# Two layer programs, each with its norms, MLP and projections, in place of nine barriered stages

## What is computed

```python
for layer in range(2):
    sh1, sc1, g1, sh2, sc2, g2 = ada(c, w_ada[layer], b_ada[layer])
    if layer == 1:
        kv = x @ w_kv                       # written out as k and v
    h = x * (1 + sc1) + sh1
    mix = pool_mixer(h) if layer == 0 else stick_breaking(h @ w_q, keys, vals) @ w_o
    x = layer_norm(ALPHA * x + g1 * mix)
    h = x * (1 + sc2) + sh2
    f = square(relu(h @ w_up[layer])) @ w_down[layer]      # 1024 -> 4096 -> 1024
    x = layer_norm(ALPHA * x + g2 * f)
```

## Time and profile before

| | |
|---|---|
| median of 3 runs | 3626.75 us (3626.16 to 3627.1) |
| the profiled execution's own time | 3627.95 us, its span 3626.2 us |
| PE busy | 3166.2 us (87% of the span) |
| DVE busy | 1961.4 us (54%) |
| ACT busy | 923.5 us (25%) |
| POOL busy | 445.2 us (12%) |

### The profile page before, as it was taken

One profiled execution on the slowest core, in us unless ns is written; L12 is line 12 of the kernel. 1 busy time (PEld: TensorE's weight loads), 2 busy tenths in 40 slices (PEclk: granted clock), 3 DMA queues, 4 the chain that ended last, 5 costly groups with the idle time before them and its releaser, 6 DMA issues. The chain is left out here.

```text
span 3626.2 us, 56133 instructions
## 1 busy us (share of the span) xinstructions
PE 3166.2 (87%) x20656; PEld 2672.9 (74%) x20656; DVE 1961.4 (54%) x3395; ACT 923.5 (25%) x1598; POOL 445.2 (12%) x248
## 2 busy tenths in 40 slices
PE   5664999999995997799899997888794999999997
PEld 1234999999994997765565654444493999999995
DVE  2566555555555112266666666888615555555554
ACT  0114000000003002144444445777504000000003
POOL 0002111212210111100000000000010221222210
PEclk8887999999997998899999998999997999999998
DMA  8711111111100221399999993000001111111101
GB/s 329 254 48 58 41 35 46 38 43 46 40 23 29 80 78 52 127 380 404 395 397 398 397 408 103 24 24 18 24 23 29 47 41 46 46 46 46 46 23 49
DMA packets 215691, 433.75 MB, mean 120 GB/s; under 512 B 13664, under 2 KB 130057, under 8 KB 212441
## 3 DMA queue, kind: packets, MB, share of 16 engines
q1 hardware_dynamic: 215521, 431.67, 32.8%
...
## 5 line engine op out<-in xcount | busy, mean ns | idle before, releaser
L84 PE MATMUL bank<-hi,mlp_uphi 128*128 128x364 f32 (+1 forms) x1536 | 506.5, 330 | 92.5 <-POOL mlp_uplo L692 92.5
L85 PE MATMUL bank<-lo,mlp_uphi 128*128 128x364 f32 (+1 forms) x1536 | 506.6, 330 | 0.0
L86 PE MATMUL bank<-hi,mlp_uplo 128*128 128x364 f32 (+1 forms) x1536 | 506.4, 330 | 0.0
L85 PE MATMUL bank<-mlp_flo,mlp_dnhi 128*128 128x364 f32 (+1 forms) x1536 | 504.8, 329 | 0.0
L84 PE MATMUL bank<-mlp_fhi,mlp_dnhi 128*128 128x364 f32 (+1 forms) x1536 | 504.7, 329 | 0.0
L86 PE MATMUL bank<-mlp_fhi,mlp_dnlo 128*128 128x364 f32 (+1 forms) x1536 | 504.7, 329 | 0.0
L302 DVE SCALAR_TENSOR_TENSOR x_t<-bank,mod,x_t 128x364 f32<-128x364 f32 (+1 forms) x432 | 245.6, 571 | 379.0 <-PE bank L86 376.7
L84 PEld LDWEIGHTS bank<-hi,mlp_uphi 128*128 128x128 f32 x1536 | 290.4, 189 | 93.6 <-POOL mlp_uplo L692 93.6
L1291 PE MATMUL bank<-ident,sa_kraw 128*128 128x128 f32 x2048 | 278.7, 281 | 58.5 <-DMA sa_kraw<-in_cache_k 53.5
L1291 PEld LDWEIGHTS bank<-ident,sa_kraw 128*128 128x128 f32 x2048 | 225.8, 142 | 111.2 <-DMA sa_kraw<-in_cache_k 83.0
L1173 DVE COPY sa_kt<-bank 128x512 f32<-128x512 f32 x256 | 177.0, 692 | 215.6 <-PE bank L1291 211.7
...
## 6 DMA issues: line engine op xcount, KB each, us to landing
sa_kraw<-in_cache_k SPq DMA_DIRECT2D x256, 512.0 KB, 10.6
sa_vpage<-in_cache_v SPq DMA_DIRECT2D x256, 512.0 KB, 9.4
mlp_raw<-in_w_up SPq DMA_DIRECT2D x64, 512.0 KB, 4.0
mlp_raw<-in_w_down SPq DMA_DIRECT2D x64, 512.0 KB, 3.5
...
pm_wada<-in_w_ada SPq DMA_DIRECT2D x48, 512.0 KB, 5.2
...
```

The costliest lines, as they stand in the source:

```text
L84: pe.matmul(out, w_hi, x_hi, start=start, stop=False, skip_group_check=True)
L85: pe.matmul(out, w_hi, x_lo, start=False, stop=False, skip_group_check=True)
L86: return pe.matmul(out, w_lo, x_hi, start=False, stop=stop, skip_group_check=True)
```

## The change

Query projection and attention are kept as they were. The other nine stages after the pool mixer become two programs, `first_layer_mlp` (n00, m0, n01, keys and values) and `second_layer_mlp` (wo, n10, m1, n11, the output), each one block with one barrier at its end. `norm` becomes a class whose steps are single calls per piece: `pe_mean`, `dve_center`, `act_square`, `pe_var`, `dve_scale`, `act_root`, `act_high` (writes `hi` and the full h from `x_t` with gain, bias and modulation folded into `coef`), `dve_split` (writes `lo`), `act_affine`. DVE's steps are done in two halves of 4 chunks. `Mlp` takes the norm before it and the norm after it and calls their steps inside its first and its last block. The up jobs are in another order (`UP`), wo goes by pieces with all its weights held, the keys and values take two weight blocks in turn by token tiles, and the norms use PSUM banks 6 and 7.

The diff, cut to its core:

```diff
+    def pe_mean(self, pe, s):
+        c0, w = PIECES[s]
+        if s == 2:
+            pe.wait_ge(self.centred, 4)
+        for m in range(NC):
+            last = pe.matmul(self.mean_bank[s][:, 0:w], self.k.mean_of[:, :], self.k.x_t[:, m, c0:c0 + w],
+                             start=(m == 0), stop=(m == NC - 1))
+        last.then_inc(self.mu, 1)
+    def pe_var(self, pe, s):
+        c0, w = PIECES[s]
+        if s == 1:
+            pe.wait_ge(self.root, 1)
+        else:
+            pe.wait_ge(self.centred, 2 * s + 2)
+        for m in range(NC):
+            if m % 4 == 0:
+                pe.wait_ge(self.squared, 2 * s + m // 4 + 1)
+            last = pe.matmul(self.var_bank[s][:, 0:w], self.k.mean_of[:, :], self.sq[:, m, c0:c0 + w],
+                             start=(m == 0), stop=(m == NC - 1))
+        last.then_inc(self.var, 1)
...
+    def dve_center(self, dve, s):
+        w = PIECES[s][1]
+        dve.wait_ge(self.mu, s + 1)
+        for half in range(2):
+            x = self.piece(self.k.x_t, s, half)
+            dve.tensor_tensor(x, x, self.mean_bank[s][:, 0:w].unsqueeze(1).to_broadcast([P, 4, w]), ALU.subtract
+                              ).then_inc(self.centred, 1)
+    def dve_scale(self, dve, s):
+        w = PIECES[s][1]
+        v = self.var_bank[s][:, 0:w]
+        dve.wait_ge(self.var, s + 1)
+        dve.tensor_scalar(v, v, EPS, None, ALU.add).then_inc(self.eps, 1)
+        dve.wait_ge(self.eps, s + 1)
+        dve.reciprocal(v, v).then_inc(self.inv, 1)
+        dve.wait_ge(self.root, s + 1)
+        for half in range(2):
+            x = self.piece(self.k.x_t, s, half)
+            dve.tensor_tensor(x, x, self.rstd[:, 0:w].unsqueeze(1).to_broadcast([P, 4, w]), ALU.mult
+                              ).then_inc(self.scaled, 1)
...
+    def act_root(self, act, s):
+        w = PIECES[s][1]
+        act.wait_ge(self.inv, s + 1)
+        if s:
+            act.wait_ge(self.scaled, 2 * s)
+        act.activation(self.rstd[:, 0:w], self.var_bank[s][:, 0:w], ACT.Sqrt).then_inc(self.root, 1)
...
+    def act_high(self, act, s):
+        k = self.k
...
+                else:
+                    scale, shift = k.coef[:, m:m + 1], k.coef[:, 8 + m:9 + m]
+                    act.activation(k.hi[:, m, c0:c0 + wp], x, ACT.Identity, bias=shift, scale=scale)
+                    last = act.activation(self.h[:, m, c0:c0 + wp], x, ACT.Identity, bias=shift, scale=scale)
+            last.then_inc(self.high, 1)
...
+    NB, FC, JOBS, BANKS, TILES = DFF // 512, 4, 36, 6, 8
+    ORDER = [("down", 0), ("up", 2), ("down", 1), ("up", 3), ("down", 2), ("down", 3), ("next", 0), ("next", 1)]
+    UP = [(0, 0), (0, 1), (1, 0), (1, 1), (0, 2), (1, 2), (2, 0), (2, 1), (2, 2), (3, 0), (3, 1), (3, 2)]
...
+    def act_rest(self, act):
+        def hi_half(i, r, kind, c):
+            used = {"down": 0, "up": 3 + c, "next": 9 + 3 * (c % 2)}[kind]
+            act.wait_ge(self.raw_in[r % 2], i * (self.TILES // 2 * 16) + 16 * ((2 + r) // 2 + 1))
+            act.wait_ge(self.job_done, i * self.JOBS + (used + 1))
+            act.activation(self.split_target(kind, c)[0], self.raw[:, r % 2, :], ACT.Copy).then_inc(self.w_hi_done, 1)
...
+        def block(i, first=False, last=False):
+            own.base, own.k = i * (36 + 16), 0
+            for j, (c, s) in enumerate(self.UP):
+                c0, w = PIECES[s]
+                if first and j == 2:
+                    before.dve_split(dve, 2)
+                dve.wait_ge(self.job_done, i * self.JOBS + (j + 2))
...
+            dve.wait_ge(self.bank_free, i * self.JOBS + (self.BANKS + 12))
+            if first:
+                dve.wait_ge(before.normed, 3)
+            for j in range(12, self.JOBS):
+                s, m = divmod(j - 12, NC)
+                dve.wait_ge(self.job_done, i * self.JOBS + (j + 2))
+                gated_add(dve, own, k, self.layer, 5, m, s, k.ps[j % self.BANKS], self.tmp, self.bank_free)
+                if last and s and m == 1:
+                    after.dve_center(dve, s - 1)
+                if last and s == 2 and m == 2 and after.to:
+                    after.dve_split(dve, 0)
+                if last and s and m == 6:
+                    after.dve_scale(dve, s - 1)
+        block(0, first=True)
+        with dve.Fori(1, self.NB - 1) as i:
+            block(i)
+        block(self.NB - 1, last=True)
...
+        def block(i, first=False, last=False):
+            for j in range(self.JOBS):
+                pe.wait_ge(self.bank_free, i * self.JOBS + (j + 1))
+                if j < 12:
+                    c, s = self.UP[j]
+                    c0, w = PIECES[s]
+                    if s == 0:
+                        pe.wait_ge(self.w_done, i * self.TILES + (2 + (1, 2, 4, 6)[c]))
+                    if first and c == 0:
+                        pe.wait_ge(before.split, s + 1)
...
+                done.then_inc(self.job_done, 1)
+                if first and j == 1:
+                    before.pe_var(pe, 2)
+                if last and j in (12 + 8 + 1, 12 + 16 + 1):
+                    s = (j - 12) // 8 - 1
+                    pe.wait_ge(self.bank_free, i * self.JOBS + (self.BANKS + 12 + 8 * s + 8))
+                    after.pe_mean(pe, s)
+                if last and j in (12 + 8 + 5, 12 + 16 + 5):
+                    after.pe_var(pe, (j - 12) // 8 - 1)
+        block(0, first=True)
+        with pe.Fori(1, self.NB - 1) as i:
+            block(i)
+        block(self.NB - 1, last=True)
+        pe.wait_ge(self.bank_free, self.NB * self.JOBS + self.BANKS)
+        after.pe_mean(pe, 2)
...
+    JOBS = ([(0, t) for t in range(5)] + [(1, t) for t in range(5)] + [(0, t) for t in range(5, 9)]
+            + [(1, t) for t in range(5, 9)])
...
+        def high_weights(act, i, n):
+            act.wait_ge(raw_in[n], i * 16 + 16)
+            act.wait_ge(job_done, i * 18 + (14 + 4 * n))
+            act.activation(weights(0, n), raw[:, n, :, :], ACT.Copy).then_inc(w_hi_done, 1)
...
+        @block.sync
+        def _(sp):
+            ff.sync(sp)
...
+            sp.wait_ge(ff.job_done, ff.jobs_until(11))
+            for n in range(2):
+                load(sp, n, slice(n * W, (n + 1) * W))
...
+            ff.act_first(act)
+            n0.act_square(act, 0)
+            n0.act_square(act, 1)
+            n0.act_root(act, 0)
+            n0.act_high(act, 0)
+            n0.act_square(act, 2)
+            n0.act_root(act, 1)
+            n0.act_high(act, 1)
+            n0.act_root(act, 2)
+            n0.act_high(act, 2)
+            n0.act_affine(act, 2)
+            n0.act_affine(act, 0)
+            n0.act_affine(act, 1)
+            ff.act_rest(act)
+            for s in range(3):
+                n1.act_square(act, s)
+                if s:
+                    act.wait_ge(ff.job_done, ff.jobs_until(12 + 8 * s + 7))
+                    high_weights(act, 0, s - 1)
+                n1.act_root(act, s)
+                n1.act_high(act, s)
+                n1.act_affine(act, s)
...
+        @block.vector
+        def _(dve):
+            n0.dve_coefficients(dve)
+            n0.dve_center(dve, 0)
+            n0.dve_center(dve, 1)
+            n0.dve_scale(dve, 0)
+            n0.dve_center(dve, 2)
+            n0.dve_scale(dve, 1)
+            n0.dve_split(dve, 0)
+            n0.dve_split(dve, 1)
+            n0.dve_scale(dve, 2)
+            ff.dve(dve)
+            n1.dve_center(dve, 2)
+            n1.dve_split(dve, 1)
+            for j in range(3):
+                keep(dve, 0, j)
+            n1.dve_scale(dve, 2)
+            for j in range(3, 8):
+                keep(dve, 0, j)
+            n1.dve_split(dve, 2)
+            for j in range(8, 18):
+                keep(dve, 0, j)
+            with dve.Fori(1, 4) as i:
+                for j in range(18):
+                    keep(dve, i, j)
...
+            n0.pe_mean(pe, 0)
+            n0.pe_mean(pe, 1)
+            n0.pe_var(pe, 0)
+            n0.pe_mean(pe, 2)
+            n0.pe_var(pe, 1)
+            ff.pe(pe)
+            for j in range(18):
+                if j in (0, 2, 10):
+                    pe.wait_ge(n1.split, (0, 2, 10).index(j) + 1)
+                if j == 3:
+                    n1.pe_var(pe, 2)
+                job(pe, 0, j)
+            with pe.Fori(1, 4) as i:
+                for j in range(18):
+                    job(pe, i, j)
...
+            for j in range(24):
+                s, m = divmod(j, NC)
+                c0, w_ = PIECES[s]
+                if s == 0:
+                    pe.wait_ge(w_done, m + 1)
+                if j >= BANKS:
+                    pe.wait_ge(bank_free, j - BANKS + 1)
...
+                if s and m == 1:
+                    pe.wait_ge(bank_free, NC * s)
+                    n0.pe_mean(pe, s - 1)
+                if s and m == 3:
+                    n0.pe_var(pe, s - 1)
+            pe.wait_ge(bank_free, 24)
+            n0.pe_mean(pe, 2)
+            ff.pe(pe)
+            pe.wait_ge(n1.normed, 1)
```

(38 more changed lines are left out.)

668 lines of the change are left out of this document (340 added, 328 removed).

## The result

The changed kernel takes **3543.14 us** (median of 4 runs, 3540.34 to 3548.3) against 3626.45 before; the ratio is 0.9772, 95% interval 0.9755 to 0.9789. The profiled execution is the slowest of the four, 3548.3 us with a span of 3546.6.

A forecast was written before the change was run, and what follows sets the result against it. TensorE was taken to bound the MLPs, with idle gaps at the norms between them to fill. 12.0 + 30.0 + 33.2 - 3.8 = 71.4 off 3627.95 gives 3556.5, forecast as 3556 us, range 3548 to 3577.

The forecast's parts named there:

- Code: TensorE's longer program, first and last blocks written out: fetching and branching cost nothing, so 0 in the sum.
- Head of layer 0: First norm to up job 6 of layer 0: up jobs start earlier, TensorE idles 13.5 us before job 4; gain 12.0.
- End of m0 to keys and values: From down job 21 of layer 0's last block: norm overlaps down jobs, keys start earlier; gain 30.0.
- wo, n10, head of m1: Output projection to up job 6 of layer 1: norm overlaps wo's jobs, wo's weights barely hide; gain 33.2.
- End to output: End of layer 1's MLP to the output: means in TensorE's row and VectorE waits outweigh the overlap; loss 3.8.
- Inner blocks: MLP blocks between first and last: chunk 2's up weight ties with job 6; 0 to 4 us in all, 0 taken.
- (a): Rival: TensorE's clock holds through the 6.9 us pauses ahead of mean 2, saving twice 2.7 us: 3551; chance 0.12.
- (b): Rival: five short TensorE pauses around norms, keys and output cost clock too, 8.5 us, so 3565; chance 0.14.
- (c): Rival: VectorE's chain is longer, above all in last blocks; up to 21 us more, middle given as 3572; chance 0.12.
- (d): Rival: inner blocks wait for the up weight, 0.3 to 1 us in 14 blocks, 3560 to 3570; chance 0.12.

The follow-up runs named there:

- e5: Changed kernel with 33 more SyncE instructions (waits already met) at the end of the q projection, moving its loop over the samples; 3557.01 us.
- e12: Changed kernel with all tried reorderings together, plus the old chunk-by-chunk up-job order in all but each MLP's first block; 3522.17 us, ratio 0.9698.
- e4: Changed kernel with VectorE's scale of the piece before behind the eighth add instead of the seventh, in each MLP's last block; 3538.17 us.

## Why the prediction was wrong, step by step

**The step that failed is "Code".** It priced the program's shape at 0, from eight iterations of TensorE's loop without idle time. That row answers for TensorE alone. Its program grew (the first instruction queue moved 84 packets before and 109 after), and the sums below leave no cost to it. It says nothing of SyncE's loop, in a stage that the diff doesn't touch and where the DMA engines are full. The change shortened SyncE's program ahead of that loop by 32 instructions, and the jump back went from 6.2 to 1.3 us: the term set at 0 measured a gain of 13.6 us. By e5 the same kernel with 33 instructions back takes 3557.0; the forecast of 3556 was that kernel's time. The other terms came out at 73.2 for 71.4. The rule of the Trainium skill that I set aside (Runtime: NRT & Kernel Launch, "Instruction fetch mechanics": a taken branch outside of the held window stalls for a fetch) agrees with the trace of SyncE's loop after all, with the 30 extra packets beside it; its block of 256 instructions does not account for the two places at 514 and 580.

**Head of layer 0**: right; 13.25 for 12.0, with job 4 at 79.1 behind the mean (79.5 forecast) and its wait 13.4 (13.5). Job 6 waits for up weight 2 as said.

**End of m0 to keys and values**: right, 29.87 for 30.0. Mean 2 starts 58.0 behind job 21 (56.9) and ends at 64.7 (64.6). The queue on VectorE is as described, the add behind the scale:

```profile
1111.77 3.26 DVE L389 TENSOR_TENSOR x_t<-x_t,norm_rstd 128x1456 f32<-128x1456 f32 x2 [0.54 <-ACT norm_rstd L427]
1114.95 0.22 DVE L286 TENSOR_TENSOR mlp_tmp<-bank,mod 128x64 f32<-128x64 f32 x1
```

**wo, n10, head of m1**: right, 33.83 for 33.2, with 15.4 us of idle ahead of job 4 (15.8).

**End to output**: the sign was right, the size not: a loss of 1.8 for 3.8. The last copy ends 90.2 behind job 21 (91.1), and 4.1 us of writes follow it instead of 6.1; I had taken 0.8 off.

**Inner blocks**: the tie tips by 0.13 a block, 1.8 to 2.0 in all, at job 6 as said, inside the 0 to 4 that were kept; e12 gives most of it back.

**The rivals.** (a) fell: mean 2 took 6.78 and 7.01 us at a granted clock of 0.68 and 0.70 after its pauses of 6.6, part of it at 1.2 GHz, and 4.68 and 4.94 in e4 after 1.01. (b) is half right: after the pauses of 1.95 mean 1 took 6.41 once (clock 0.73) and 4.72 once (1.00), and var 2 of n11 after 1.56 took 4.95 (1.00). So a short pause cost 1.7 us in one of three places. Windows on those means in the changed kernel:

```profile
1085.79:1092.20 6.41, 6.41 (x17) 3.76 (x17) 1.53 (x6) 6.38 (x12) 0.00 (x0) 0.73 0.01 3
1115.92:1122.70 6.78, 6.78 (x17) 4.08 (x17) 0.00 (x0) 6.75 (x12) 0.00 (x0) 0.68 0.00 0
3480.11:3484.83 4.72, 4.72 (x16) 2.98 (x17) 1.53 (x6) 4.23 (x8) 0.00 (x0) 1.00 0.00 0
3508.74:3515.75 7.01, 7.01 (x16) 4.18 (x17) 0.00 (x0) 3.90 (x7) 0.00 (x0) 0.70 0.01 2
```

(c) and (d) with more than 0.3 a block did not come; (c)'s price was also mis-stated, for up to 21 us on top of 3556 has its middle at 3567 and not at 3572. With what was measured in place of the terms, the sum is 73.2 + 13.6 = 86.8, and 3627.95 - 86.8 = 3541.2; the nine runs of the changed kernel lie from 3540.3 to 3548.3.
